# Reordered operand sums in a fast-product MLP, four wide norm roots, and a last product by token tiles, in a two-layer encoder trunk on one core

## The reference

```python
def rmsnorm(x, g):
    xf = x.astype(jnp.float32)
    y = xf * lax.rsqrt(jnp.mean(xf * xf, axis=-1, keepdims=True) + EPS)
    return (y * g.astype(jnp.float32)).astype(x.dtype)
...
def squared_relu_mlp(h, w1, w2):          # w1: (1024, 4096), w2: (4096, 1024)
    return jnp.square(jax.nn.relu(h @ w1)) @ w2
...
    for i in range(DEPTH):                # DEPTH = 2
        ...
        h = rmsnorm(x, norm_mem_g[i])
        m = rmsnorm(mem, norm_memkv_g[i])
        x = x + mem_attention(h, m, mem_w_q[i], mem_w_kv[i], mem_w_o[i])
        h = rmsnorm(x, norm_ffn_g[i])
        x = x + squared_relu_mlp(h, ffn_w1[i], ffn_w2[i])
    return rmsnorm(x, final_norm_g)
```

## Time and profile before

| | |
|---|---|
| median of 3 runs | 1201.26 us (1200.92 to 1202.06) |
| profiled execution | 1201.64 us, its span 1199.8 us |
| busy share PE / DVE / ACT / POOL | 97% / 64% / 43% / 16% |
| mean granted TensorE clock | 0.991 of full speed |
| PE's idle time before L1841, ended by DVE `s_lo` L1029 | 18.1 us in 10 waits, the longest 5.9 us |
| HBM read, written | 148.28 MB, 2.10 MB |

### The profile page before, as it was taken

How to read it: one execution, slowest core, us unless ns; L and a number is a source line. 1 busy time by engine, 2 the same in 40 slices (tenths; PEclk the granted TensorE clock), 3 DMA queues, 4 the chain that set the end, 5 groups by cost and what they waited for, 6 DMA issues and landing times.

```text
span 1199.8 us, 13648 instructions
## 1 busy us (share of the span) xinstructions
PE 1163.9 (97%) x5392; PEld 966.9 (81%) x5392; DVE 765.4 (64%) x918; ACT 516.1 (43%) x688; POOL 196.9 (16%) x147
## 2 busy tenths in 40 slices
PE   9999999999999999799999999999999999999975
PEld 7888888878878788688888888888887878878864
DVE  7786665575585575676488655657557557566576
ACT  7654433344343343454444433433235334344344
POOL 0040053010010100112254062006201010010010
PEclk9999999999999999999999999999999999999988
DMA  9432142464565555425223522105437546556261
GB/s 364 176 106 88 36 180 90 134 133 152 122 158 155 116 147 158 82 60 174 79 97 115 201 76 99 59 32 210 122 89 158 156 110 156 149 111 176 39 103 73
DMA packets 41536, 151.28 MB, mean 126 GB/s; under 512 B 4736, under 2 KB 4864, under 8 KB 40832
## 3 DMA queue, kind: packets, MB, share of 16 engines
q1 hardware_dynamic: 30960, 113.26, 26.9%
q0 software_dynamic: 9216, 33.56, 16.5%
q10 hardware_dynamic: 1296, 3.58, 0.9%
HBM read 148.28 MB, written 2.10 MB: 125 GB/s over the span
## 4 chain that ended last, share of the span: by engine, by line
PE 81%; DVE 7%; DMA 4%; ACT 4%; issue 3%; POOL 0%; SPq 0%; ACTq 0%; DVEq 0%; POOLq 0%
PE psum L1583 20%; PE psum L1585 20%; PE psum L1584 20%; PE psum L1841 7%; PE psum L1842 6%; PE psum L1843 6%; DMA w_sum<-in_down 3%; ACT w_hi L641 1%; DMA w_raw<-in_weights 1%; DVE w_lo L1014 1%; DVE s_lo L1029 1%; ACT w_hi L628 1%; DVE w_lo L1005 1%; DVE z L1245 1%; PE psum L1771 1%
## 5 line engine op out<-in xcount | busy, mean ns | idle before, releaser
L1583 PE MATMUL psum<-a_lo,w_hi 128*128 128x512 f32 x704 | 276.7, 393 | 0.0
L1585 PE MATMUL psum<-a_hi,w_lo 128*128 128x512 f32 x704 | 274.3, 390 | 0.0
L1584 PE MATMUL psum<-a_hi,w_hi 128*128 128x512 f32 x704 | 274.2, 389 | 0.0
L1014 DVE TENSOR_TENSOR w_lo<-w_sum,w_hi 128x1024 fp32r<-128x1024 f32 x112 | 136.8, 1224 | 96.8 <-ACT w_hi L641 96.7
L1002 DVE TENSOR_TENSOR w_lo<-w_raw,w_hi 128x1024 fp32r<-128x1024 f32 x122 | 154.5, 1270 | 65.9 <-ACT w_hi L628 65.8
L1841 PE MATMUL psum<-w_lo,s_hi 128*128 128x512 f32 x448 | 177.2, 396 | 18.1 <-DVE s_lo L1029 18.1
L1842 PE MATMUL psum<-w_hi,s_hi 128*128 128x512 f32 x448 | 176.0, 393 | 0.0
L1843 PE MATMUL psum<-w_hi,s_lo 128*128 128x512 f32 x448 | 176.0, 393 | 0.0
L1584 PEld LDWEIGHTS psum<-a_hi,w_hi 128*128 128x128 f32 x704 | 132.3, 188 | 27.9 <-issue 1.0
L1583 PEld LDWEIGHTS psum<-a_lo,w_hi 128*128 128x128 f32 x704 | 132.2, 188 | 27.8 <-issue 1.0
L1585 PEld LDWEIGHTS psum<-a_hi,w_lo 128*128 128x128 f32 x704 | 132.2, 188 | 27.7
(11 more groups left out here) (175 smaller groups left out, 1708.7 us busy)
## 6 DMA issues: line engine op xcount, KB each, us to landing
w_raw<-in_weights SPq DMA_DIRECT2D x154, 512.0 KB, 3.6
w_sum<-in_down POOLq DMA_DIRECT2D x64, 512.0 KB, 5.3
w_sum<-in_down SPq DMA_DIRECT2D x48, 512.0 KB, 4.4
x<-in_x_t SPq DMA_DIRECT2D x2, 1024.0 KB, 8.2
x_tok<-in_x_rows SPq DMA_DIRECT2D x2, 1024.0 KB, 7.6
...
out_rows<-out_rows SPq DMA_DIRECT2D x2, 512.0 KB, 2.6
...
```

What stands on the lines that cost most here:

```text
L1014: dve.tensor_tensor(w_lo[:, c % RING, :], w_sum[:, SUM_BUFFER[part] + half, :], w_hi[:, c % RING, :].bitcast(F32), ALU.subtract).then_inc( ...
L1583: pe.matmul(out_ap, s_hi, m_lo, start=start, stop=False)
L1584: pe.matmul(out_ap, s_hi, m_hi, start=False, stop=False)
L1585: return pe.matmul(out_ap, s_lo, m_hi, start=False, stop=stop)
```

## The change

Six edits. In each MLP block the sums S1b and S2 are made one behind the other, S2 ahead of the weight split for N0 (D5 in the last block), and S4 ahead of the splits for D5 and D6 (D6 and D7 in the last block); A12b's split now stands behind S2's, and the order of a few splits on ACT is changed to fit, with hidden tiles 6 and 7 squared later. In the four norms named above the sum and the spreading are one matmul of 128x512 (`totals`), and ACT and DVE take the root on 128x512 (`wide_sd`, `wide_root`); `sums` and `bcast` stay for the norm of the gating mixer. In the last block of layer 1 D12 and D13 are done for the first token tile and then for the second. One `gained` moves ahead of the reading of P7. The final norm takes the roots of tiles 0 and 1 together, tile 1 is scaled by DVE instead of ACT, and the per-tile steps of tiles 2 and 3 are reordered.

```diff
         for b in range(FB):
             for name in steps_of(b):
-                if name == "D13" and b == FB - 1:
-                    if l == 0:
-                        for m in range(4, 8):
-                            self.add(("xt", m), "ready")
-                    else:
-                        self.add(("last", 0), "ready")
+                if name == "D13" and (l, b) == (0, FB - 1):
+                    for m in range(4, 8):
+                        self.add(("xt", m), "ready")
+                if name == "D12" and (l, b) == (1, FB - 1):
+                    self.add(("last", 0), "ready")
+                    continue
...
+
+            def wide_sd(n, key):
+
+                act.wait_ge(sums_ready, n)
+                act.activation(sq[:, 0, :], bank(key), ACT.Sqrt, bias=eps[:], scale=1.0 / D).then_inc(sd_ready, 1)
 
...
                     hi_ahead(l, b, "U6")
-                    h_tile(b, 6)
                     summed(b, 2)
                     slot_free(b - 1, "D10")
                     hi(s_hi[:, 1, 0:2], act_h[:, 0:2, TOK[1]])
                     hi_ahead(l, b, "U7")
+                    h_tile(b, 6)
+                    hi_ahead(l, b, "D1")
                     h_tile(b, 7)
-                    hi_ahead(l, b, "D1")
                     summed(b, 3)
                     hi(s_hi[:, 1, 2:4], act_h[:, 2:4, TOK[1]])
                     hi_ahead(l, b, "D2")
+                    summed(b, 4)
+                    slot_free(b - 1, "D13")
+                    hi(s_hi[:, 2], act_h[:, 0:4, TOK[0]])
                     own_h(b, 7)
                     hi(s_hi[:, 3, 2:4], act_h[:, 6:8, TOK[0]])
                     hi_ahead(l, b, "D3")
-                    summed(b, 4)
-                    slot_free(b - 1, "D13")
-                    hi(s_hi[:, 2], act_h[:, 0:4, TOK[0]])
                     hi_ahead(l, b, "D4")
-                    if more:
-                        hi_ahead(l, b, "N0")
                     summed(b, 5)
                     slot_free(b, "D1")
                     hi(s_hi[:, 0], act_h[:, 4:8, TOK[0]])
+                    if more:
+                        hi_ahead(l, b, "N0")
                     hi_ahead(l, b, "D5")
                     slot_free(b, "D4")
...
+                act.wait_ge(lastbias_ready, 1)
                 for t in range(2):
                     row_root(t)
-                    act.wait_ge(scaled_ready, 3)
-                    scaled_out(t, slice(0, 1024), out_ready[0])
+                act.wait_ge(lasty_ready, 1)
+                squares(2, 0)
+                row_root(2)
+                act.wait_ge(scaled_ready, 3)
+                scaled_out(0, slice(0, 1024), out_ready[0])
+                act.wait_ge(lasty_ready, 2)
+                squares(3, 0)
+                row_root(3)
                 for t in range(2, ST):
-                    act.wait_ge(lasty_ready, t - 1)
-                    act.wait_ge(lastsq_ready, t + 3)
-                    squares(t, 0)
-                    row_root(t)
                     scaled_out(t, COLS[1], out_ready[2])
 
...
+            def wide_root(n, key):
+
+                dve.wait_ge(sd_ready, n + 1)
+                dve.reciprocal(z[:, 0, :], sq[:, 0, :]).then_inc(root_step, 1)
+                dve.tensor_scalar(sq[:, 1, :], bank(key), 1.0 / D, EPS, ALU.mult, ALU.add).then_inc(taken, 1)
+                root_steps[0] += 1
+                dve.wait_ge(root_step, root_steps[0])
+                dve.tensor_tensor(z[:, 1, :], z[:, 0, :], z[:, 0, :], ALU.mult).then_inc(root_step, 1)
+                root_steps[0] += 1
+                dve.wait_ge(root_step, root_steps[0])
+                dve.wait_ge(taken, N.bank[key] + 1)
+                dve.scalar_tensor_tensor(out=z[:, 1, :], in0=z[:, 1, :], scalar=-0.5, in1=sq[:, 1, :],
+                                         op0=ALU.mult, op1=ALU.mult).then_inc(root_step, 1)
+                root_steps[0] += 1
+                dve.wait_ge(root_step, root_steps[0])
+                dve.scalar_tensor_tensor(out=rstd[:], in0=z[:, 1, :], scalar=1.5, in1=z[:, 0, :],
+                                         op0=ALU.add, op1=ALU.mult).then_inc(rtok_ready, 1)
+                dve.wait_ge(rtok_ready, n + 1)
...
@@ -1308,36 +1335,37 @@
                     lo_ahead(l, b, "U5")
                     relu(b, 5)
                     lo_ahead(l, b, "U6")
-                    lo_part(b, "A12a", 3, LEFT, act_h[:, 4:6, TOK[0]])
                     h_done(b, 5)
                     summed(b, 1)
                     dve.tensor_tensor(act_h[:, 0:2, TOK[1]], act_h[:, 4:6, TOK[1]], act_h[:, 0:2, TOK[1]],
                                       ALU.subtract).then_inc(s_step, 1)
+                    lo_part(b, "A12a", 3, LEFT, act_h[:, 4:6, TOK[0]])
+                    lo_part(b, "S1a", 1, LEFT, act_h[:, 0:2, TOK[1]])
                     relu(b, 6)
-                    lo_part(b, "S1a", 1, LEFT, act_h[:, 0:2, TOK[1]])
                     lo_ahead(l, b, "U7")
                     relu(b, 7)
                     lo_ahead(l, b, "D1")
                     h_done(b, 7)
                     dve.tensor_tensor(act_h[:, 2:4, TOK[1]], act_h[:, 6:8, TOK[1]], act_h[:, 2:4, TOK[1]],
                                       ALU.subtract).then_inc(s_step, 1)
-                    lo_ahead(l, b, "D2")
-                    read(b, "P1", "D1", (0, 0), False, after=before(b, "P1", 2))
-                    lo_part(b, "S1b", 1, RIGHT, act_h[:, 2:4, TOK[1]])
-                    lo_ahead(l, b, "D3")
-                    lo_part(b, "A12b", 3, RIGHT, act_h[:, 6:8, TOK[0]])
                     summed(b, 3)
                     dve.scalar_tensor_tensor(out=act_h[:, 0:4, TOK[0]], in0=act_h[:, 0:4, TOK[1]], scalar=-1.0,
                                              in1=act_h[:, 0:4, TOK[0]], op0=ALU.mult, op1=ALU.subtract).then_inc(s_step, 1)
-                    lo_ahead(l, b, "D4")
+                    lo_part(b, "S1b", 1, RIGHT, act_h[:, 2:4, TOK[1]])
+                    lo_ahead(l, b, "D2")
                     lo_part(b, "S2", 2, ALL, act_h[:, 0:4, TOK[0]])
+                    read(b, "P1", "D1", (0, 0), False, after=before(b, "P1", 2))
+                    lo_part(b, "A12b", 3, RIGHT, act_h[:, 6:8, TOK[0]])
+                    dve.wait_ge(lo_ready, N.lo[key(b, "A12b")] + 1)
                     summed(b, 4)
                     dve.scalar_tensor_tensor(out=act_h[:, 4:8, TOK[0]], in0=act_h[:, 4:8, TOK[0]], scalar=-1.0,
                                              in1=act_h[:, 0:4, TOK[0]], op0=ALU.mult, op1=ALU.subtract).then_inc(s_step, 1)
+                    lo_ahead(l, b, "D3")
+                    lo_ahead(l, b, "D4")
+                    lo_part(b, "S4", 0, ALL, act_h[:, 4:8, TOK[0]])
                     if more:
                         lo_ahead(l, b, "N0")
                     read(b, "P5", "D4", (1, 1), True, after=before(b, "P7", 7))
-                    lo_part(b, "S4", 0, ALL, act_h[:, 4:8, TOK[0]])
                     if more:
                         relu(b + 1, 0)
...
+                        dve.wait_ge(gain_loaded, 16)
+                        gained(0, 1, "P3")
                     read(b, "P7", "D10", (1, 1), True, after=key(b, "P5"))
                     if more:
...
-                for t in range(2, ST):
-                    dve.wait_ge(psum_ready, (N.ready["f1", b, "D13"] if t == ST - 1 else N.ready["last", 0]) + 1)
-                    dve.tensor_tensor(y_rows[:, t, COLS[0]], y_rows[:, t, COLS[0]], bank(("last", t - 2)),
-                                      ALU.add).then_inc(lasty_ready, 1)
-                for t in range(2, ST):
-                    row_scale(t)
-                    dve.wait_ge(lastr_ready, t + 1)
-                    dve.scalar_tensor_tensor(out=out_rows[:, t, COLS[0]], in0=y_rows[:, t, COLS[0]], scalar=last_r[:, t:t + 1],
-                                             in1=last_gain[:, COLS[0]], op0=ALU.mult, op1=ALU.mult).then_inc(out_ready[1], 1)
+                gained(0, 0, "P2")
+                last_sum(2, N.ready["last", 0])
+                row_scale(0, 2)
+                dve.wait_ge(lastr_ready, 1)
+                dve.wait_ge(scaled_ready, 3)
+                dve.tensor_scalar(out_rows[:, 1, :], out_rows[:, 1, :], last_r[:, 1:2], None, ALU.mult).then_inc(out_ready[3], 1)
+                last_sum(3, N.ready["f1", b, "D13"])
+                row_scale(2, 1)
+                dve.wait_ge(lastr_ready, 2)
+                row_scale(3, 1)
+                first_columns(2, 2)
+                first_columns(3, 3)
 
             attention(0, 2)
...
+            def totals(key, norm):
+
+                wait_bank(key)
+                pe.wait_ge(ssq_step, SUMMED[norm])
+                pe.matmul(bank(key), ones[:], ssq[:], start=True, stop=True).then_inc(sums_ready, 1)
+
...
                     c = step(l, b, name)
                     pe.wait_ge(wlo_ready, c + 1)
                     if need is not None:
...
+                    if len(tiles) == 2 or name == "D13":
```

(6 more changed lines are left out.)

85 lines of the change are left out of this document (40 added, 45 removed).

## The result

The changed kernel takes 1172.66 us (median of 4 runs, 1172.51 to 1173.31); before took 1201.66 us beside it (4 runs, 1200.92 to 1202.09). The ratio is 0.976, with a 95% interval of 0.9743 to 0.9777. The forecast was 1173.6 us. The profiled execution after took 1173.31 us, its span 1171.4 us: the span is 28.4 us shorter. By the medians the change is worth 29.0 us, since before's median is 0.4 us higher here than the 1201.26 of the forecast.

The account below looks back on a forecast made before the run. PE, busy in 97% of the span, was taken as the bound. D4 waits 6.4, last blocks 7.75 and 5.8, norms 3.7 and tail 4.1 make 27.7 us off 1201.26: 1173.6 us, range 1169 to 1179.

Parts of the forecast that it names:

- The waits ahead of D4 and D5: MLP blocks: all ten PE waits for `s_lo` go; D4's cost 1.06 us each, D5's 8.65.
- the 8.65 us of the earlier trace: Last blocks: cost of D5's 5.9 us wait together with the slow matmuls at 1.2 GHz behind it.
- What is late next: Last block of each layer: D9 waits for weights from the second of two adds, cost 1.95 us.
- the rival that the adds do not hold each other: Rival in the last blocks: the two adds run independently, D9 waits for nothing, 1169.8 us; chance 0.17.
- The falling clock: Rival in the last blocks: the clock falls after the new waits, 4.2 us back, 1177.8 us; chance 0.12.
- D12: Last block of layer 1: D12 waits for P7's reading behind the moved `gained`, cost 1.05 us.
- The norms: Four norms: PE saves 0.92 us each, 3.7 in all, with the wide reciprocal priced at 0.7.
- slow reciprocal: Rival in layer 0's attention: the wide reciprocal is slow, scores wait up to 2 us, 1175.6 us; chance 0.07.
- The tail: From PE's end to the span's end: 12.9 us become 8.8, gain 4.1.

Follow-up runs that it names:

- e2_old_sums: The changed kernel with the order of sums and splits in the MLP blocks on DVE and ACT as before; 1194.16 us.
- e12_small_add: The changed kernel with the add ahead of D9's, in each last block, moving 64 of 1024 columns, the rest left out; 1170.63 us.
- e9_swap_adds: The changed kernel with D9's add issued ahead of the one that waits for D6's split, in each last block; 1175.58 us.
- e4_gained_behind: The changed kernel with the one moved `gained` put behind the reading of P7; 1173.28 us.
- e1_narrow_norms: The changed kernel with the four norms as before (one-column sums, root on 128x4); 1177.75 us.
- e5_p6_first: The changed kernel with the reading of P6 ahead of the split of D9's weights in each last block; 1171.88 us.
- e8_no_reciprocal: The changed kernel with the four norms' wide reciprocal replaced by a multiply-add writing a constant; 1172.56 us.

## Why the prediction was right

**The waits ahead of D4 and D5.** All ten went, as the step-by-step order of DVE said; e2_old_sums puts them back with their price. The six D4 gained 1.08 each where 1.06 was taken from the earlier trace rows. The clock's part in the 8.65 us of the earlier trace rows came back with the wait.

**What is late next.** D9 was named, with its cause: the second add behind the first, landing 8.3 us after the first one's issue. It landed 8.1 (layer 1) and 8.3 (layer 0) after it. The wait cost 1.63 and 1.80, not 1.95. e12_small_add and e9_swap_adds show the cause from both sides: with a sixteenth of the data ahead 1.3 us go, and with D9's add first its landing is the 5.2 of the earlier trace rows. So the rival that the adds do not hold each other is out. The Trainium skill, "DMA: Bandwidth & Descriptors", section "Queues, rings and completion order", says that each engine consumes descriptors in ring order. These rows agree; but the page says it of the queues of SP and ACT, and it adds that a later descriptor may finish its write before an earlier one, so that it is the rows that show it for POOL's adds.

**The falling clock**, a rival with 0.12, is no mechanism of the usual execution, but it is real: e4_gained_behind and e1_narrow_norms show it in the profiled executions in which the add landed 1.0 and 1.4 us later than in after. In e5_p6_first it landed 0.8 us later, and the clock stayed at 1.00. The profiled execution of after shows a clock of 1.00 behind all three waits, and the four runs spread over 0.8 us, less than the 2.6 to 3.0 that the fall cost.

**D12** was sized 1.05 and cost 0.89, and e4_gained_behind shows no gain in the time when it is gone. The working holds this already, unsaid: the end hangs on DVE's 6.8 us behind the reading of P7 and not on D12, so what D12 loses in one term comes off the tail in the other. With the `gained` behind the reading, that reading is 1.14 sooner and DVE's chain behind it 1.14 longer.

**The norms** were mis-sized in one term and nearly right in another. PE's saving is 0.95 us a norm (0.92 taken). The wide reciprocal was priced at 0.7 us from the 168 ns of four columns beside a multiply-add of 170, and that is the term that was wrong. DVE's timeline of after, in the norm ahead of layer 0's attention:

```profile
89.37 3.35 DVE L1087 RECIPROCAL z<-sq 128x512 f32<-128x512 f32 x1 [1.04 <-ACT sq L663]
92.64 0.63 DVE L1088 TENSOR_SCALAR sq<-psum 128x512 f32<-128x512 f32 x1
...
94.62 0.69 DVE L1099 SCALAR_TENSOR_TENSOR rstd<-z 128x512 f32<-128x512 f32 x1
```

It takes 3.35 us; all four are the same. That is 4.9 times the 0.69 of the multiply-add of two tensors behind it, and 7.9 times the 0.43 of the multiply-add by constants that stands in its place in e8_no_reciprocal. So `rstd` stood at 95.3 and not at 92.8, against 95.6 before: the margin was 0.3 us. The scores (99.62) waited 0.25 us for a split of q, and 0.3 more came back right behind, 0.55 where the rival "slow reciprocal" had up to 2; e8_no_reciprocal gets 0.57 back. The other three norms hide it behind a whole tile, as forecast. The step that failed goes from four columns to 512: the multiply-add grew from 170 to 427 ns, the reciprocal from 168 to 3353, so the row of four columns says nothing of the price per column. In the Trainium skill, "VectorE: DVE Perf Modes", section "First, the fixed hardware budget", `Reciprocal` is an iterative division with a repeat count of 8. The direction was right, and it had a chance of 0.07. As an estimate from that page, eight passes of 0.69 us would be 5.5 and eight of 0.43 would be 3.4; 3.35 was measured, and no run tells whether a repeat is such a pass.

**The tail** was sized 8.8 behind PE's end and took 8.3. DVE's timeline of after:

```profile
1161.02 0.68 DVE L1435 TENSOR_TENSOR y_rows<-y_rows,psum 128x512 f32<-128x512 f32 x1
...
1162.85 0.75 DVE L1453 TENSOR_SCALAR out_rows<-out_rows,last_r 128x1024 f32<-128x1024 f32 x1
1163.52 0.68 DVE L1435 TENSOR_TENSOR y_rows<-y_rows,psum 128x512 f32<-128x512 f32 x1
...
1166.17 1.41 DVE L1441 SCALAR_TENSOR_TENSOR out_rows<-y_rows,last_r,last_gain 128x512 f32<-128x512 f32 x2
```

Tile 1's scaling of 1024 columns takes 0.75 us, less than the 0.9 assumed, and the two last roots together 2.1 (1164.11 to 1166.17) where 2.6 was taken from one root of before that held a wait of its own. Tile 3's sum starts 0.4 us behind PE's end, not 1.1. Against these stands a term that was too small: the end of the span comes 3.8 us behind the last column step, not 3.1. SP now issues four stores one after the other and the last of them only at 1168.3:

```profile
1166.94 1.80 SPq L615 DMA_DIRECT2D out_rows<-out_rows  x4
```

That DVE and not PE is last is as forecast.

The errors have both signs: the norms gave 0.4 less, the two last blocks 0.55 more and the tail 0.5 more, itself 1.2 too long in one place and 0.7 too short in another. That the sum was off by only 0.7 of 28.4 us owes something to that, which is luck and not the working.
